# Two attention layers: latent rotations as two streams, two gate blocks moved to the dilated attention, and a new way of spreading the dense steps

## The reference

```python
for l in range(2):
    proj = rms_norm(x, attn_norm[l]) @ w_in[l]
    a_q, a_k, a_v, b_ql, b_kvl, b_kr, c_q, c_k, c_v, gate = split(proj)
    # A: dilated attention, 12 heads of 64, norm of each head, part of it rotated
    aq = partial_rope(rms_norm(a_q)); ak = partial_rope(rms_norm(a_k))
    o_a = dilated_mixture(aq, ak, a_v)
    # B: latent attention, 8 heads of 96, the last 32 of each rotated
    bq = rms_norm(b_ql) @ w_q_b[l]; kv = rms_norm(b_kvl) @ w_kv_b[l]
    bk = concat(k_nope, b_kr for every head)
    bq = rope(rms_norm(bq)); bk = rope(rms_norm(bk))
    o_b = causal_softmax(bq, bk, bv)
    # C: stick-breaking attention, 8 heads of 64
    o_c = stick_breaking(c_q, c_k, c_v)
    g = sigmoid(gate)                      # 3 x 1024 columns
    x = x + (g0 * (o_a @ wa) + g1 * (o_b @ wb) + g2 * (o_c @ wc)) @ w_out[l]
    x = x + square(relu(rms_norm(x) @ w_ff1[l])) @ w_ff2[l]
```

## Time and profile before

| | before |
|---|---|
| median of three runs | 5403.37 us (5393.2 to 5405.93) |
| profiled execution | 5405.11 us |
| its span | 5403.3 us |
| PE busy | 4835.4 us, 89% of the span |
| DVE busy | 2127.8 us, 39% |
| ACT busy | 1301.5 us, 24% |

### The profile page before, as it was taken

One profiled execution on the slowest core, in us unless ns is written; L12 is line 12 of the kernel. 1 busy time (PEld: TensorE's weight loads), 2 busy tenths in 40 slices (PEclk: granted clock), 3 DMA queues, 4 the chain that ended last, 5 costly groups with the idle time before them and its releaser, 6 DMA issues.

```text
span 5403.3 us, 80212 instructions
## 1 busy us (share of the span) xinstructions
PE 4835.4 (89%) x33872; PEld 2948.3 (55%) x33872; DVE 2127.8 (39%) x3904; ACT 1301.5 (24%) x2400; POOL 426.1 (8%) x386
## 2 busy tenths in 40 slices
PE   8899999988988969979887997999998997999999
PEld 2466666676554544453233554544777554544777
DVE  2455555553354451031112236363333236363333
ACT  0233333332222210010001133231222123232222
POOL 0011111110231230000000000010000000010000
PEclk9899999998989979989998997999999997999999
DMA  6000000001101022127997110113221210113221
GB/s 247 27 18 18 18 18 18 4 5 45 39 32 47 16 100 115 70 91 324 419 418 293 71 53 20 59 55 126 106 94 52 85 53 20 48 59 130 109 94 47
DMA packets 70701, 494.63 MB, mean 92 GB/s; under 512 B 8771, under 2 KB 9027, under 8 KB 29251
## 3 DMA queue, kind: packets, MB, share of 16 engines
q1 hardware_dynamic: 70342, 489.49, 23.4%
HBM read 468.47 MB, written 21.00 MB: 91 GB/s over the span
## 4 chain that ended last, share of the span: by engine, by line
PE 75%; DVE 9%; issue 8%; DMA 5%; ACT 2%; POOL 1%; SPq 0%; DVEq 0%; POOLq 0%; PEldq 0%; ACTq 0%; PEld 0%
PE ps L224 72%; DMA upper<-in_ew 4%; PE ps L227 3%; DVE upper L235 2%; ACT upper L282 1%; DVE upper L243 1%; DVE upper L259 1%; DVE lower L235 1%; POOL upper L3250 1%; DVE lower L243 1%; DVE upper L251 1%; DVE upper L239 1%; DMA lower<-in_ada 0%; ACT lower L282 0%; DVE upper L255 0%
## 5 line engine op out<-in xcount | busy, mean ns | idle before, releaser
L224 PE MATMUL ps<-lower 128*128 128x512 f32 (+10 forms) x6512 | 1958.2, 466 | 94.4 <-issue 25.1
L224 PEld LDWEIGHTS ps<-lower 128*128 128x128 f32 (+3 forms) x6512 | 1010.2, 198 | 852.3 <-issue 668.3
L224 PE MATMUL ps<-upper 64*64 64x64 f32 (+7 forms) x14224 | 913.6, 261 | 148.5 <-DVE upper L251 42.9
L282 ACT ACTIVATE upper<-ps 128x512 f32<-128x512 f32 (+6 forms) x963 | 445.6, 483 | 2094.8 <-PE ps L224 1432.3
L224 PEld LDWEIGHTS ps<-upper 64*64 64x64 f32 (+4 forms) x14224 | 653.9, 150 | 466.1 <-issue 247.4
L224 PE MATMUL ps<-lower,upper 64*64 64x64 f32 (+6 forms) x7216 | 818.4, 326 | 73.7 <-DMA lower<-in_ew 27.5
L224 PE MATMUL ps<-rounded 128*128 128x512 f32 x3072 | 719.8, 396 | 30.6 <-DVE rounded L235 23.1
L224 PEld LDWEIGHTS ps<-rounded 128*128 128x128 f32 x3072 | 583.1, 190 | 166.5 <-ACT rounded L282 26.3
L224 PEld LDWEIGHTS ps<-lower,upper 64*64 64x64 f32 (+3 forms) x7216 | 415.0, 146 | 415.0 <-issue 360.0
L224 PE MATMUL ps<-upper,lower 128*128 128x512 f32 (+4 forms) x1200 | 507.3, 571 | 16.3 <-DVE lower L243 5.6
L282 ACT ACTIVATE upper<-upper 128x768 f32<-128x768 f32 (+10 forms) x615 | 323.6, 531 | 677.8 <-POOL upper L3250 144.4
(11 more groups left out here) (78 smaller groups left out, 2112.1 us busy)
## 6 DMA issues: line engine op xcount, KB each, us to landing
lower<-in_ew SPq DMA_DIRECT2D x144, 1024.0 KB, 12.0
upper<-in_ew SPq DMA_DIRECT2D x48, 1024.0 KB, 13.7
lower<-in_b0f SPq DMA_DIRECT2D x16, 2048.0 KB, 8.1
lower<-in_b1f SPq DMA_DIRECT2D x16, 2048.0 KB, 7.7
lower<-in_ada SPq DMA_DIRECT2D x12, 2048.0 KB, 9.4
lower<-in_wrkv SPq DMA_DIRECT2D x8, 1728.0 KB, 7.3
lower<-in_b0g SPq DMA_DIRECT2D x8, 1536.0 KB, 6.6
gad<-upper SPq DMA_DIRECT2D x48, 256.0 KB, 2.0
```

Source lines behind the costliest of these rows:

```text
L224: return self.e.matmul(out, lhsT, rhs, start=start, stop=stop)
L282: self.e.activation(out, in_, func, bias=bias, scale=scale, accum_out=accum).then_inc(line.up(*event), 1)
```

## The change

Four things change in `block2_order()`, with what the programs need for them.
- `latent()` ends after the `kv` steps. The rotations of B are two generators of their own, `latent_rope(0)` for the queries and `latent_rope(1)` for the keys, each of which waits (yields nothing) until its tile is in `made`. The keys' stream has semaphores of its own (`k.step[1]`, used before by the rotations of A) in place of those of the team `tail`. In the list of generators the latent ones now come ahead of the lanes.
- Five gate blocks instead of three lie ahead of softB, and three instead of five behind it; the order of the weight loads follows.
- `drain` gives out dense steps after each step of a generator and not after each round: each step adds n to `due`, and while `due` is at least 1 a dense step is put into the list. A generator that waits adds nothing.
- n is 2 for each step (it was 4 for each round of two generators) in the rotations of A, 0.25 (1 for each round) in softA, 0.4 (2) in softB and 0.25 (2) in stick.

```diff
--- before.py
+++ after.py
@@ -2338,7 +2338,7 @@
 
 
 def block2_order():
-    ready, turned, out = set(), set(), []
+    ready, turned, made, out = set(), set(), set(), []
 
     def tok(t):
         for i in range(4):
@@ -2361,7 +2361,7 @@
             for t in ts:
                 yield from tok(t)
             ready.add(name)
-        yield from gates(range(3))
+        yield from gates(range(5))
 
     def half(par):
         for w in range(2):
@@ -2390,11 +2390,17 @@
         for i in range(4):
             for n in range(2):
                 yield ("bq", i, n)
+            made.add((0, i))
             for n in range(2):
                 yield ("kv", i, n)
-        for j in range(8):
+        made.update((1, i) for i in range(4))
+
+    def latent_rope(w):
+        for i in range(4):
+            while (w, i) not in made:
+                yield None
             for s in range(4):
-                yield ("brope", j, s)
+                yield ("brope", 2 * i + w, s)
 
     def mixture():
         for s in range(7):
@@ -2408,37 +2414,40 @@
             yield None
         yield from tok("c2")
         ready.add("c")
-        yield from gates(range(3, 8))
+        yield from gates(range(5, 8))
 
     def drain(gens, other, n):
-        gens = list(gens)
+
+        gens, due = list(gens), 0.0
         while gens:
             for g in list(gens):
                 step = next(g, 0)
                 if step == 0:
                     gens.remove(g)
-                else:
+                elif step is not None:
                     out.append(step)
-            for _ in range(n):
-                out.append(next(other, None))
+                    due += n
+                while due >= 1:
+                    out.append(next(other, None))
+                    due -= 1
 
     out += tok("a0")
     out += tok("a1")
     filler = dense()
-    drain([half(0), half(1)], filler, 4)
+    drain([half(0), half(1)], filler, 2)
     while "lat" not in ready:
         out.append(next(filler))
     out.append(("meet", "A"))
-    drain([lane("softA", 48, 4, z) for z in range(6)] + [latent()], filler, 1)
+    drain([latent(), latent_rope(0), latent_rope(1)] + [lane("softA", 48, 4, z) for z in range(6)], filler, 0.25)
     out += filler
     out.append(("meet", "latent"))
     out += [("bT", s, z) for s in range(2) for z in range(8)]
     filler = dense_c()
-    drain([lane("softB", 32, 4, z) for z in range(6)] + [mixture()], filler, 2)
+    drain([lane("softB", 32, 4, z) for z in range(6)] + [mixture()], filler, 0.4)
     while "c" not in ready:
         out.append(next(filler))
     out.append(("meet", "B"))
-    drain([lane("stick", 32, 5, z) for z in range(6)], filler, 2)
+    drain([lane("stick", 32, 5, z) for z in range(6)], filler, 0.25)
     out += filler
     out.append(("meet", "C"))
     return [s for s in out if s is not None]
@@ -2507,9 +2516,9 @@
         fetch(sp, k.c2b, T["c2"], "c2")
     ring = Ring(sp, [k.wreg[:, 4096 * i:4096 * i + 4096] for i in range(2)])
     loads = [(t, P.pe, "tok", l, t, 3) for t in ("a0", "a1", "a2", "a3", "a4", "a5", "b0")]
-    loads += [(f"g{d}", P.pe, "gate", l, d, 2) for d in range(3)]
+    loads += [(f"g{d}", P.pe, "gate", l, d, 2) for d in range(5)]
     loads += [(t, P.pe, "chan", l, t, 3) for t in ("c0", "c1")] + [("c2", P.pe, "tok", l, "c2", 3)]
-    loads += [(f"g{d}", P.pe, "gate", l, d, 2) for d in range(3, 8)]
+    loads += [(f"g{d}", P.pe, "gate", l, d, 2) for d in range(5, 8)]
     loads = iter([((l, t), b2_source(T, l, t), *until) for t, *until in loads] +
                  [((l, "br", d), T[f"b{l}br"][d], M.pe, "branch", l, d, 2) for d in range(8)] +
                  [((l, "o", n), T[f"b{l}o"][n], M.pe, "oproj", l, 3, n) for n in range(2)] +
@@ -2965,7 +2974,7 @@
             i, w = j // 2, j % 2
             if s == 1 and w:
                 v.wait_ge(tail.pool, "bk", l, i)
-            heads_vector(k, v, l, tail, (b.bq, b.bkk)[w][:, i, :], 96, b.gains[2 + w], 64, 16, c2["cosm"], c2["sinm"], i,
+            heads_vector(k, v, l, (tail, k.step[1])[w], (b.bq, b.bkk)[w][:, i, :], 96, b.gains[2 + w], 64, 16, c2["cosm"], c2["sinm"], i,
                          b.sq[w], b.sts[w], s, ("brope", l, j))
         elif name == "mix":
             mix(*z)
@@ -3143,8 +3152,8 @@
                 else:
                     a.wait_ge(tail.dve, "bq", l, i, 1)
                 if j > 1:
-                    a.wait_ge(tail.dve, "brope", l, j - 2)
-            heads_scalar(k, a, tail, (b.bq, b.bkk)[w][:, i, :], 96, b.sq[w], b.sts[w], s, ("brope", l, j))
+                    a.wait_ge((tail, k.step[1])[w].dve, "brope", l, j - 2)
+            heads_scalar(k, a, (tail, k.step[1])[w], (b.bq, b.bkk)[w][:, i, :], 96, b.sq[w], b.sts[w], s, ("brope", l, j))
         elif name == "mix":
             s, = z
             sq = b.sq[0]
```

## The result

| | before | after |
|---|---|---|
| median | 5403.72 us (5393.2 to 5405.93, 4 runs) | 5345.75 us (5340.84 to 5346.24, 4 runs) |
| ratio | 1 | 0.9894, 95% interval 0.9877 to 0.9912 |
| span of the profiled execution | 5403.3 us | 5344.4 us |

The changed kernel is 58 us faster.

A forecast was written before the change was run, and what follows sets the result against it. TensorE, busy 89%, was taken to bound the kernel by work, waits and low clock. Per layer -10.7 + 17.2 + 3.6 - 35 = -25, -50 for both, giving 5356 us; bounds -42 to +5 a layer, range 5333 to 5392.

The forecast's parts named there:

- What bounds: Whole kernel: TensorE, busy 89% of the span; time is its work, its waits and its low clock; only the last two can move.
- The arithmetic of softA: softA and latent: work 199.7 us, waits 7, low clock 3, tail 9, together 218.7 against 201.5, +17.2 a layer.
- The unit work of stick: stick: 172.4 us less waits, clock loss and 56 dense steps leaves 52.1 us of TensorE work for the units.
- Up to meet A: Before meet A: seven gate steps fewer, -12.2 us, with 1.5 of exposed copy added, sum -10.7 us a layer.
- softB: softB: two more dense steps, waits left as they were, +3.6 us a layer (2 to 7).
- stick: stick: with 30 dense steps instead of 56, 172.4 us falls to 137, -35 us a layer (-22 to -42).
- the hole: End of softA: TensorE stands still for 31.0 us while only rotations of B are left; to shrink to about 9.
- the slow stretch: The 32.6 us ahead of the hole in softA: no dense steps left, TensorE busy 29.0 us at mean clock 0.52.
- rival 2: stick: TensorE falls to 1.2 GHz for most of the stage, +10 in place of -35 us, 5445; chance 0.08.
- GpSimd beside VectorE: stick: shared way to SBUF gives more side-by-side instructions in a shorter stage, 4 us a layer at most.
- Rival 1: stick: VectorE's bursts become waits, stage stays near 160 us, -12 instead of -35, 5401; chance 0.13.
- Rival 3: softA: VectorE falls behind, three rotations left over, +10 us a layer, 5376; chance 0.79 together with the forecast.

The follow-up runs named there:

- one stream: The changed kernel with the latent rotations as one chain behind the kv steps again: 5361.0 us, ratio 0.9919.
- stick_bare: The changed kernel with all eight gate blocks ahead of softB (0.385 dense steps for each step in softA) and no dense work in stick: 5418.1 us, ratio 1.0039.
- stick_spread: The kernel before with only stick's 56 dense steps given out by step (0.36 for each) instead of two after each round: 5360.2 us, ratio 0.9926.
- stick_even: The changed kernel with stick's 30 dense steps spread over all its 160 steps (0.19), not the first 120 (0.25): 5319.8 us, ratio 0.9850.
- gates_only: The kernel before with five gate blocks instead of three ahead of softB and the order of their loads, nothing else: 5383.6 us, ratio 0.9963.
- spread_only: The kernel before with dense steps given out by step, not by round; three gate blocks ahead of softB, one latent chain: 5328.6 us, ratio 0.9865.
- streams_only: The kernel before with the two latent streams alone, gates and drain as before: 5405.9 us, ratio 1.0004.
- four_late: four_gates with softA's 47 dense steps held back until the rotations start (0.1 for each step, then 0.225): 5289.0 us, ratio 0.9801.
- four_gates: The changed kernel with four gate blocks ahead of softB instead of five (0.19 in softA, 0.27 in stick): 5295.7 us, ratio 0.9805.

## Why the prediction was right

The forecast was 5356 and 50 us less; it came to 5345.75 and 58 less. Step by step:

- **What bounds** (TensorE's work, its waits, its low clock): this is an accounting and fits every run; what can be wrong is the size of its terms. The arithmetic of softA is the best part: 218.7 forecast, 219.3 measured; 203 and 202.5 for gates alone, 229 and 228.4 for one stream (there by luck, see above). The unit work of stick, 52.1 us, is 50.7 in stick_bare and 150.3 - 101.4 = 48.9 in stick_spread.
- **Up to meet A**: -10.7 forecast, -12.4 measured. The copy behind the last rotation cost nothing (the wait at the meet fell from 0.88 to 0.37 us).
- **softB**: +3.6 forecast, -1.8 measured. I added two dense steps and left the waits as they were; they fell from 6.1 to 2.6 us. The spacing goes with it: each kernel with the new `drain` has 139.0 us here (stick_bare, without gate steps in softB, apart), each with the old one 140.5 to 140.8. Two layers of this are 11 us, the largest net miss of the sum.
- **stick**: -35 forecast, -37 measured, but by luck: two larger errors offset each other. I had 110.4 us for the first 120 steps, 16 of them waits; they took 98.5, with 5 of waits. I took 27 us for the last 40 steps; they took 36.8. The sign that I named, 16 us or more of waits on VectorE, didn't come: over the whole stage they are 9 us, and 6 more on ScalarE. The step that failed is "for waits I take 16, twice today's": it takes today's waits as the price of the stage's content, when they were the price of the spacing. stick_spread shows it: the same content goes from 172.4 to 152.0 us. Of the 37 us, 20 are spacing, and taking 26 steps away adds 17, though they are 47 us of TensorE's work. (Were the 30 steps spread to the end, taking 26 away would add 27, from 152.0 to 125.2; the bare end costs 10 of them.)
- **Where the gain comes from.** The first paragraph of the prediction says that the hole and the slow stretch are all that can be won. It is wrong: stick_spread leaves both as they were (its hole is 31.00 us too) and is some 40 us faster. The three parts don't add: alone they give 0 (streams), 20 (gates) and 75 us (spreading), and together 58. With the spreading and the streams in place, the move of two blocks as the change makes it wins nothing (ratios 0.9885 without and 0.9894 with it, the attention of the two layers 12 us longer). That is the fault of stick's bare end and not of the move: with the 30 steps of stick spread to its end (stick_even, 0.9850) it wins 17 us. The move of one block wins 41 us (0.9805).
- **The clock** (rival 2): low clock is found in the tail of stick, the second half of gates_only's, and stick_bare as a whole (0.54, 0.59 and 0.50), each time in a stretch of unit steps with short waits and no dense work. As long as dense steps are mixed in one by one, even 30 over 160, the clock of stick stays at 0.94 or more (but at 0.89 in spread_only's last 21 us, where they run out). Rival 2 had the place and not the extent: 37 us of the stage in place of two thirds. The Trainium skill ("TensorE: Matmul & The Clock Gate", section "HAM oscillation — how this bites in real kernels") says that repeated waits between short groups of matmuls bring the clock down again each time. These three rows, with waits of at most 2.7 us, don't contradict it, but streams_only does not need it: 25.5 us at 0.50 with 0.4 us of waits. What in the unit steps goes with the low clock, their narrow matmuls or their transposes, the runs don't separate.
- **GpSimd beside VectorE**: the estimate of 4 us a layer for more overlap in a shorter stick isn't seen. VectorE was busy for 99.2 us in stick before and for 96.6 after, and that is the four copies of 0.69 us that it has less (17 and 13 of 128x512); the 128x128 operation of the earlier trace rows went from 595 to 593 ns. Yet the contention itself is there, and the mean hides it. Of the 16 instructions of that group five take 1.27 or 1.28 us and the others 0.28 or 0.29. Before, each of the five starts 0.13 or 0.14 us behind a GpSimd instruction of 128x512, and the two end together to within 0.15 us; the others run beside none. First VectorE's, then GpSimd's:

```profile
3505.47 1.27 DVE L243 SCALAR_TENSOR_TENSOR upper<-upper 128x128 f32<-128x128 f32 x1
3510.68 0.28 DVE L243 SCALAR_TENSOR_TENSOR upper<-upper 128x128 f32<-128x128 f32 x1
...
3505.34 1.27 POOL L3250 TENSOR_TENSOR upper<-upper 128x512 f32<-128x512 f32 x1 [4.34 <-DVE upper L2884]
```

The stages of after and of stick_bare have five such pairs too, each 1.27 us. So a shorter stage has no more of this cost, where the estimate let it grow.

- **Rival 1** (stick stays near 160): excluded. **Rival 3** (rotations left over): the tail's waits are 10.1 us, 9 forecast.
- **Slips of the sum**: the bounds given for softA's terms add up to +8 to +34, where the prediction goes on with +10 to +29, and those for stick's to -46 to -10, where it has -42 to -22. By its own terms the bounds added up are -48 and +22 us a layer, not -42 and +5. The highest DMA share in the earlier trace rows is 0.19, not 0.21. The forecast doesn't rest on these.

In short, the places and the sum were right, and what makes a thin stage slow was not. That a score matmul waits in softA for a bank that VectorE has not emptied is read from the releaser alone (L243 is what empties a score's bank); more banks for the units weren't tried. The fastest kernels here are four_late and four_gates, each beside its own runs of before: ratios 0.9801 and 0.9805, with intervals that overlap.

## What to carry to other kernels

When filler work is woven into latency-bound work, its spacing can matter as much as its amount: one filler after every few steps kept TensorE fed and at full clock, where the same fillers in a lump at the end of each round cost 12% of the stage. Let the fillers last to the very end of the stage (in stick worth 10 us a layer), and judge the split between stages by what one filler adds there, not by its own duration. Hiding a serial chain pays only where there is filler to cover the waits it makes: the same edit was worth nothing with 28 and with 35 dense steps around it, 6 to 7 us a layer with 47, and 9 with 59 (the 28 by the old rule of `drain`, the others by the new one).

## What the runs showed that I had not expected

Dense work in stick is free up to some 30 steps, and comes near its own price, 1.8 us a step, only beyond some 42 (0.6 us a step from 30 to 42, 1.4 from 42 to 56). Spread over the stage, 0, 30, 42, 54 and 56 steps took 127.8, 125.2, 132.1, 154.0 and 152.0 us, for 0, 54, 76, 98 and 101 us of added TensorE work. The small matmuls of the units alone, busy 79% of the time with waits of at most 2.5 us, ran at 1.2 GHz throughout; with 30 evenly placed dense steps the clock was 0.94 to 0.97. The dense steps paid for themselves in two ways: for 54 us more work TensorE was busy for only 10.7 us more, and it stood still for 13.1 us in place of 26.4. (That 56 took 2 us less than 54 goes with their ends: the 54 run out ten unit steps before the stage does, with 4.4 us of standing still and a clock of 0.89 in the last 21 us, the 56 four steps before, at 1.00 to the end.)
